# A hybrid encoder trunk on one core: GpSimd held back behind VectorE in the S5 prefix, and the mixer's head loop reordered

## The reference, cut to what matters

```python
proj = xn @ w_in                     # u (512), xm (512), v (512), o_pre (512)
y_a = s5_group(u, ...)               # 32 groups of 16 channels, 64 complex states each
q, k = per-head products of silu(conv4(xm)); v from proj; input and forget gates from q, k, v
h_t = mlstm_chunkwise(q, k, v, gates)         # 4 heads of 128
y_b = sigmoid(o_pre) * rmsnorm(h_t)
return concat(y_a, y_b) @ w_out
```

## Time and profile before

| | us |
|---|---|
| median of 3 runs (lowest, highest) | 1081.69 (1081.07, 1082.23) |
| the profiled execution's own time | 1083.43 |
| its span in the profile | 1081.6 |
| PE busy | 1068.1 |
| DVE, ACT, POOL busy | 639.7, 463.8, 188.1 |
| DMA, mean rate | 99 GB/s |

### The profile page before, as it was taken

One profiled execution on the slowest core, in us unless ns is written; L12 is line 12 of the kernel. 1 busy time (PEld: TensorE's weight loads), 2 busy tenths in 40 slices (PEclk: granted clock), 3 DMA queues, 4 the chain that ended last, 5 costly groups with the idle time before them and its releaser, 6 DMA issues.

```text
span 1081.6 us, 15533 instructions
## 1 busy us (share of the span) xinstructions
PE 1068.1 (99%) x5556; PEld 865.7 (80%) x5556; DVE 639.7 (59%) x874; ACT 463.8 (43%) x732; POOL 188.1 (17%) x243
## 2 busy tenths in 40 slices
PE   9999999999999999999999999999999999999997
PEld 7887578888888888888888777888888888888886
DVE  6799754566666666633334775656666666643332
ACT  6455565444434343422233565553444344422221
POOL 8999720400000000000000222310000000000000
PEclk9999999999999999999999999999999999999998
DMA  6551024232222222222324111223222222222322
GB/s 228 166 126 41 20 84 175 78 117 98 97 97 97 97 97 97 97 98 99 108 94 156 60 51 50 98 97 99 96 97 97 97 97 97 97 98 97 117 78 78
DMA packets 36459, 107.27 MB, mean 99 GB/s; under 512 B 7808, under 2 KB 10112, under 8 KB 36160
## 3 DMA queue, kind: packets, MB, share of 16 engines
q1 hardware_dynamic: 36416, 106.69, 29.7%
HBM read 102.09 MB, written 3.15 MB: 97 GB/s over the span
## 4 chain that ended last, share of the span: by engine, by line
PE 88%; DVE 2%; issue 1%; POOL 0%; ACT 0%; DVEq 0%
PE bank L1569 28%; PE bank L1570 27%; PE bank L1571 27%; PE bank L1593 1%; PE bank L1957 1%; PE bank L1934 1%; PE bank L1779 1%; PE bank L1714 1%; DVE wlo L1037 1%; PE bank L1707 0%; PE bank L1742 0%; PE bank L1736 0%; POOL pbuf L670 0%; DVE outb L1540 0%; DVE wbuf L1226 0%
## 5 line engine op out<-in xcount | busy, mean ns | idle before, releaser
L1569 PE MATMUL bank<-xhi,whi 128*128 128x512 f32 x960 | 376.5, 392 | 0.1
L1570 PE MATMUL bank<-xlo,whi 128*128 128x512 f32 x960 | 373.8, 389 | 0.0
L1571 PE MATMUL bank<-xhi,wlo 128*128 128x512 f32 x960 | 373.7, 389 | 0.0
L1037 DVE TENSOR_TENSOR wlo<-raw,whi 128x1024 fp32r<-128x1024 f32 x177 | 233.4, 1320 | 209.2 <-ACT whi L687 208.7
L687 ACT ACTIVATE whi<-raw 128x1024 fp32r<-128x1024 f32 x177 | 187.0, 1057 | 327.2 <-PE bank L1571 304.8
L1569 PEld LDWEIGHTS bank<-xhi,whi 128*128 128x128 f32 x960 | 180.3, 188 | 39.4 <-issue 0.8
L1571 PEld LDWEIGHTS bank<-xhi,wlo 128*128 128x128 f32 x960 | 180.3, 188 | 37.9
L1570 PEld LDWEIGHTS bank<-xlo,whi 128*128 128x128 f32 x960 | 180.4, 188 | 37.2 <-issue 0.3
L1569 PE MATMUL bank<-ahi,whi 128*128 128x512 f32 (+1 forms) x374 | 142.4, 381 | 0.0
L1570 PE MATMUL bank<-alo,whi 128*128 128x512 f32 (+1 forms) x374 | 142.2, 380 | 0.0
L1571 PE MATMUL bank<-ahi,wlo 128*128 128x512 f32 (+1 forms) x374 | 142.2, 380 | 0.0
(11 more groups left out here) (258 smaller groups left out, 1057.4 us busy)
## 6 DMA issues: line engine op xcount, KB each, us to landing
raw<-wstream SPq DMA_DIRECT2D x177, 512.0 KB, 3.2
xin<-xT SPq DMA_DIRECT2D x8, 256.0 KB, 5.4
raw<-wstream SPq DMA_DIRECT2D x8, 256.0 KB, 5.0
h<-xT SPq DMA_DIRECT2D x1, 2048.0 KB, 8.5
u_scratch<-uperm SPq DMA_DIRECT2D x1, 1024.0 KB, 5.5
uc<-u_scratch SPq DMA_DIRECT2D x8, 128.0 KB, 4.9
bandsb<-band SPq DMA_DIRECT2D x1, 1024.0 KB, 4.8
outT<-outb SPq DMA_DIRECT2D x2, 512.0 KB, 2.9
```

The costliest lines, as they stand in the source:

```text
L1037: V.tensor_tensor(wlo[:, t % RING, :], raw[:, t % RAWS, :], whi[:, t % RING, :].bitcast(f32), ALU.subtract).then_inc(lo_done, 1)
L1569: MM(dst, wh, rhi, start=start, stop=False)
L1570: MM(dst, wh, rlo, start=False, stop=False)
L1571: return MM(dst, wl, rhi, start=False, stop=stop)
```

## The change

- POOL waits for `lo_done` 17 (tiles 15 and 16 split) before it starts turning; and, in the forward turn of half 1, between `tprod` and `uprod`, for `hms_added` 1 (`head_sum(0)`).
- `toep` is cleared in three parts: blocks 4, 5 by ACT after head 1's decays (`toep_mid`), blocks 6, 7 and then 0 to 3 by POOL. SP issues the Toeplitz DMAs in the order 5, 4, 7, 6, 3, 2, 1, 0, each group behind its part.
- DVE adds the skip diagonal right after the copy of `ksb`, reading the bank; `peak` moves to bank 6 and the transposed `acol` to bank 5.
- `out_gate(1)` moves up between the forget scan and its use; `turned_half(0)`, `(1)` move up ahead of the `acol` copy, `turned_half(3)` behind `turned_half(2)`, `out_gate(3)` ahead of `weights(1)`.
- In the head loop `head_sum` follows `head_floor` and comes ahead of `weights`, and `mask_decay` comes behind `weights`; `split_lo` of tile 18 moves from the pass of head 1 to the pass of head 2, behind `weights` of the next head.
- PE projects tile 16 between `head_scores(0)` and `head_scores(1)`.
- At the start DVE, not ACT, rounds the first half of tile 0.

```diff
@@ SP
-        sp.wait_ge(toep_clear, 1)
-        for t in range(CH):
-            sp.dma_start(toep[(CH - 1 - t) * GCH:P, t, :, :],
-                         ksb[0:(t + 1) * GCH, :, :]).then_inc(toep_built, 16)
+        for ts, free, need in (((5, 4), toep_mid, 1), ((7, 6), toep_clear, 1), ((3, 2, 1, 0), toep_clear, 2)):
+            sp.wait_ge(free, need)
+            for t in ts:
+                sp.dma_start(toep[(CH - 1 - t) * GCH:P, t, :, :],
+                             ksb[0:(t + 1) * GCH, :, :]).then_inc(toep_built, 16)
@@ POOL
-        def turned_by(dst, src, back):
+        def turned_by(dst, src, back, after_sum=0):
             tt(tprod[:, :, :, :], src, turn[:, 0:1, :, :].to_broadcast([P, 2, PAIRS, HALF_CH]), ALU.mult)
+            if after_sum:
+                pool.wait_ge(hms_added, after_sum)
...
         pool.wait_ge(s5in_copied, 2)
+        pool.wait_ge(lo_done, T_QK + RING + 1)
...
-            turned_by(part[b], xr[:, b], False).then_inc(scan_done, 1)
+            turned_by(part[b], xr[:, b], False, after_sum=b).then_inc(scan_done, 1)
...
-        G.memset(toep[:, :, :, :], 0.0).then_inc(toep_clear, 1)
+        G.memset(toep[:, 6:8, :, :], 0.0).then_inc(toep_clear, 1)
+        G.memset(toep[:, 0:4, :, :], 0.0).then_inc(toep_clear, 1)
@@ ACT
-            A(whi[:, t, part], raw[:, t % RAWS, part], ACT.Copy).then_inc(hi_done if k % 2 else half_hi, 1)
+            if k:
+                A(whi[:, t, part], raw[:, t % RAWS, part], ACT.Copy).then_inc(hi_done if k % 2 else half_hi, 1)
...
+            if hd == 0:
+                act.wait_ge(scan_done, 1)
+                A(toep[:, 4:6, :, :], ones[:, 0:GCH].unsqueeze(1).unsqueeze(1).to_broadcast([P, 2, GROUPS, GCH]), ACT.Copy,
+                  scale=0.0).then_inc(toep_mid, 1)
@@ DVE
+        dve.wait_ge(half_in[0], 16)
+        V.tensor_copy(whi[:, 0, 0:512], raw[:, 0, 0:512]).then_inc(first_hi, 1)
...
-        V.tensor_copy(ksb[:, :, :], bank[6][:, :].rearrange("p (g i) -> p g i", i=GCH)).then_inc(k_copied, 1)
+        k_rows = bank[6][:, :].rearrange("p (g i) -> p g i", i=GCH)
+        V.tensor_copy(ksb[:, :, :], k_rows).then_inc(k_copied, 1)
+        dve.wait_ge(k_copied, 1)
+        dve.wait_ge(skip_set, 1)
+        V.tensor_tensor(ksb[0:GCH, :, :], k_rows[0:GCH], skipb[:, :].rearrange("p (g i) -> p g i", i=GCH),
+                        ALU.add).then_inc(k_final, 1)
...
                                       ALU.mult, ALU.add))
+        out_gate(1)
         settle()
...
-        out_gate(1)
+        turned_half(0)
+        turned_half(1)
         dve.wait_ge(acol_ready, 1)
...
         mask_decay(0)
-        turned_half(0)
-        turned_half(1)
-        dve.wait_ge(k_copied, 1)
-        dve.wait_ge(skip_set, 1)
-        V.tensor_tensor(ksb[0:GCH, :, :], ksb[0:GCH, :, :], skipb[:, :].rearrange("p (g i) -> p g i", i=GCH),
-                        ALU.add).then_inc(k_final, 1)
         out_gate(2)
         weights(0)
         turned_half(2)
+        turned_half(3)
+        out_gate(3)
         weights(1)
-        out_gate(3)
         weights(2)
-        turned_half(3)
         mask_decay(1)
...
             weights(SB * hd + 1)
             head_floor(hd - 1)
+            head_sum(hd - 1)
+            weights(SB * hd + 2)
             if hd + 1 < HEADS:
                 mask_decay(hd + 1)
-            head_sum(hd - 1)
-            weights(SB * hd + 2)
             head_scale(hd - 1)
             weights(SB * hd + 3)
-            if hd == 1:
-                split_lo(T_O + hd + RING)
             if hd + 1 < HEADS:
                 weights(SB * (hd + 1))
+            if hd == 2:
+                split_lo(T_O + 1 + RING)
             head_gate(hd - 1)
@@ PE
         broadcast_max(0)
+        head_scores(0)
+        project(T_O + 3, O_O + 3)
         pe.wait_ge(acol_copied, 1)
-        head_scores(0)
         head_scores(1)
-        project(T_O + 3, O_O + 3)
```

More of the change, by code:

```diff
@@ L262, in build @@
     half_in = [sem(f"half_in{t}") for t in range(RING)]
-    gain_in, half_hi, half_lo = sem("gain_in"), sem("half_hi"), sem("half_lo")
+    gain_in, first_hi, half_hi, half_lo = sem("gain_in"), sem("first_hi"), sem("half_hi"), sem("half_lo")
     hi_done, lo_done = sem("hi_done"), sem("lo_done")
@@ L310, in build @@
     radius_done, radius_set, min_done = sem("radius_done"), sem("radius_set"), sem("min_done")
-    arow_done = sem("arow_done")
+    arow_done, toep_mid = sem("arow_done"), sem("toep_mid")
     turned, turned_scan, carry_done, skip_set = (sem(n) for n in (
@@ L1059, in _ @@
             t, part = k // 2, slice(512 * (k % 2), 512 * (k % 2) + 512)
-            dve.wait_ge(hi_done if k % 2 else half_hi, t + 1)
+            dve.wait_ge(*((hi_done, t + 1) if k % 2 else (half_hi, t) if k else (first_hi, 1)))
             V.tensor_tensor(wlo[:, t, part], raw[:, t % RAWS, part], whi[:, t, part].bitcast(f32),
@@ L1194, in _ @@
         dve.wait_ge(kt_ready, 1)
-        V.tensor_copy(ksb[:, :, :], bank[6][:, :].rearrange("p (g i) -> p g i", i=GCH)).then_inc(k_copied, 1)
+        k_rows = bank[6][:, :].rearrange("p (g i) -> p g i", i=GCH)
[4 more added lines that the diff above has]
+                        ALU.add).then_inc(k_final, 1)
         dve.wait_ge(lnf_done, 1)
         dve.wait_ge(vtok_copied, HEADS)
-        lf_p, a_p, peak = bank[7][f_rows, :], bank[7][0:HEADS, :], bank[5][0:HEADS, :]
+        lf_p, a_p, peak = bank[7][f_rows, :], bank[7][0:HEADS, :], bank[6][0:HEADS, :]
         V.scalar_tensor_tensor(out=lf_p, in0=bank[0][f_rows, :], scalar=0.0, in1=lf,
@@ L1213, in _ @@
         V.tensor_tensor(fcum[:, :], peak, fcum[:, :], ALU.add).then_inc(sum_rows, 1)
-        out_gate(1)
+        turned_half(0)
+        turned_half(1)
         dve.wait_ge(acol_ready, 1)
-        V.tensor_copy(acol[:, :, :], bank[4][:, 0:SB * HEADS].rearrange("p (s h) -> p s h", h=HEADS)
+        V.tensor_copy(acol[:, :, :], bank[5][:, 0:SB * HEADS].rearrange("p (s h) -> p s h", h=HEADS)
                       ).then_inc(acol_copied, 1)
@@ L1604, in _ @@
                 pe.wait_ge(xhi_done, b + 1)
-                pe.wait_ge(hi_done if b % 2 else half_hi, t + 1)
+                pe.wait_ge(*((hi_done, t + 1) if b % 2 else (half_hi, t) if b else (first_hi, 1)))
                 for m in range(4):
@@ L1700, in _ @@
         for s in range(SB):
-            ins = transpose(bank[4][:, s * HEADS:(s + 1) * HEADS], arow[:, s * P:(s + 1) * P], HEADS)
+            ins = transpose(bank[5][:, s * HEADS:(s + 1) * HEADS], arow[:, s * P:(s + 1) * P], HEADS)
         ins.then_inc(acol_ready, 1)
```

## The result

| | before | after |
|---|---|---|
| median, us | 1081.69 | 1086.48 (1085.89 to 1087.73, 5 runs) |
| ratio, 95% interval | 1 | 1.0047 (1.0036 to 1.0059) |
| profiled execution: own time, span | 1083.43, 1081.6 | 1087.73, 1086.0 |

The change makes the kernel 4.8 us slower by the medians (3.9 to 6.4 by the interval). The forecast was 1081.4, its range ended at 1083.3. The traced execution of the changed kernel is the slowest of its five, 1.25 us over their median.

The account below looks back on a forecast made before the run. PE bounds the kernel, busy 1068.1 of 1081.6 us. Toeplitz start -1.95 plus clock +1.7 gives -0.25: profiled 1083.43 becomes 1083.2, and with the median 1.74 lower, 1081.4 us; range 1079.0 to 1083.3.

Parts of the forecast that it names:

- no wait at `broadcast_max`: Mixer prefix: PE's wait of 1.42 us goes whole, and with it the slow stretch that lost 1.7 us.
- the clock falling there: At the Toeplitz products: PE's stand of 2.9 us brings a 3.5 us stretch at half clock, 1.7 us lost.
- nothing for the first weights: Kernel start: DVE's copy makes PE's first matmul about 0.5 us earlier, lost again in the wait at 28.5; 0 taken.
- the last begins 4.45 later and, being the smallest now, lands in 2.0: Toeplitz DMAs: first issued at 139.5, last begins 4.45 us later and takes 2.0 us, landing at 145.9.
- The rule on ring order: Toeplitz DMAs: tile 20's 512 KB would delay blocks behind it; products start at most at 146.2, gain falls to 1.5 us.
- my own 145.7: Forecast start of the Toeplitz products, 1.95 us earlier than the 147.66 of the profiled execution.
- (a): Rival: PE's stand at the Toeplitz products costs no clock; 1079.7 us, chance 0.17.
- (b): Rival: the Toeplitz blocks are not late, so PE's whole 4.9 us gain passes on; 1076.8 us, chance 0.13.
- the 142.8 of my working: End of the head loop: PE ready for `s5_output(0)` at 142.8 where it was at 147.66, 4.9 us gained.
- (c): Rival: slower, the clock falls twice or for twice as long at the Toeplitz products, 3.4 us lost; 1083.2 us, chance 0.10.
- (d): Rival: POOL's remainder of head 0 comes ahead of tile 18's split, all lands 1.3 us later; 1082.7 us, chance 0.05.
- (e): Rival: POOL's wait is passed before DVE comes to its splits; ruled out beforehand, no time or chance given.

Follow-up runs that it names:

- g1: The kernel before, run again unchanged for a second trace: 1081.1 us, ratio 0.9998.
- e1: The changed kernel with the split of tile 18 back in the pass of head 1: 1078.42 us, ratio 0.9975.
- f4: The changed kernel, with SP waiting until all eight Toeplitz blocks have landed before it loads tile 21: 1086.39 us, ratio 1.0046.
- e2: The changed kernel, with the load of tile 20 behind the eight Toeplitz DMAs in SP's list, split still late: 1078.5 us, ratio 0.9975.
- e3: The changed kernel, with SP waiting until tile 20 has landed before it issues the first Toeplitz DMA: 1088.06 us, ratio 1.0068.
- e4: The changed kernel, with the Toeplitz blocks issued in the order 0 to 7, all behind the last clear: 1087.02 us, ratio 1.0048.
- f2: The kernel before, with only the split of tile 18 moved to the pass of head 2: 1088.71 us, ratio 1.0064.
- g2: The changed kernel, with SP waiting for tile 20 before the first Toeplitz block and for all blocks before loading tile 21: 1087.87 us, ratio 1.006.
- h1: The kernel before, with only the floor and sum of each finished head moved ahead of the next mask: 1080.87 us, ratio 0.9998.

## Why the prediction was wrong

**Right, by the trace (1.14 us taken off).** The forget sums start at 103.23 - 1.14 = 102.1, as said; the two splits take 2.36 together; no wait at `broadcast_max`, full clock behind it; head 1 at 125.5 (said 125.3), and later heads within 0.5 us of the working; the split of tile 18 done at 138.5 (said 139.1), the load of tile 20 ahead of the blocks, PE's longest wait moved to the Toeplitz products, the clock falling there, nothing for the first weights. The mechanism and its place were right. That the clock cost 1.5 to 1.7, with 1.7 said, is luck: the low clock lasted 6.8 us, not 3.5, and half of it fell into a wait of 6.9, not 2.9.

**The step that failed** is "the last begins 4.45 later and, being the smallest now, lands in 2.0". It began where I had it (145.05 - 1.14 = 143.9, said 143.95, with one issue of 1.00 us in place of 0.6 making up for an earlier start) and landed in 5.30: 3.3 us too few. I priced the blocks from the earlier trace rows, where tile 20 had landed before they were written, and stated that difference. I then took the 2.0 anyway, since tile 20 "should land at 142.5, earlier than the last block". That compared one arrival with another; the landings of the seven blocks before it (4.1 to 4.8 us) show that all of them were held up, the last one included. The rule on ring order, which I had priced at 0.5 us, pointed the right way, at a sixth of the size. Both ends of an unseen price should have gone into the range: one tile's 3.3 us on top of its end is 1086.6.

**The second error is the base.** I worked from one profiled execution and took its 1.74 us over the median for a constant. It was the slow stretch and the wait before it (g1's span is 2.3 us shorter). Against the median the changed kernel had no wait and no slow stretch to remove: the products stood at 145.26, so my own 145.7 was already 0.4 later, not 1.95 earlier. With that, the same working gives 1081.1 + 0.4 + 1.7 = 1083.2, and with the landing of 5.3 for 2.0 and 0.2 from my rounding down, 1086.7. Measured: 1086.48. So close a match is in part luck, since the 5.3 is from an execution of 1087.73, 1.25 us over the median; its late start (29.68 at tile 4, where the traces of e1 and f4 have 28.77 and 29.27) may be 0.4 to 0.9 of that. As spans it closes to 0.1: 1079.3 (g1) to 1086.0 is 6.7; the products' start moved by 5.1 us (0.7 of which was there at tile 4 already, 28.97 to 29.68), and the clock costs 1.5.

**The rivals.** (a) fell: the clock did fall. (b) held in the kernels that free the blocks (e1, e2), where I had 1076.8 and the runs show 1078.4; the difference is again the base (145.26 to the 142.8 of my working is 2.5 us, and 2.7 were measured). (c), slower, came out in sign and in the clock: it was low for twice as long as in the earlier trace rows, from 147 to 153.8. But half of that lay inside the wait, so it cost 1.5 and not 3.4, and most of the loss is the wait of 6.9, which (c) does not have. (d) did not occur: the split came ahead of POOL's remainder. (e) did not occur: POOL stood 3.28 us for the split.

**Open.** In all six traces in which PE stands at the Toeplitz products (after, e3, e4, f2, f4, g2) one of the eight issues on SP takes 0.70 to 2.23 us in place of 0.6, and in the other eight traces none does. What makes it is not shown. A candidate is the packet of 16 KB that the profile lists as "q8 instruction": in e3, e4, f2 and g2 one was under way during the slow issue (143.75 to 145.50 in e4), in after and f4 it came behind the slow issue, while blocks were still landing (146.22 and 144.77), and in the other eight traces all blocks had landed before it. It may also have held up the last block after the change. Nor is it shown how much of the 5.30 belongs to the one traced execution.

## What to carry to other kernels

Moving work that frees a buffer moves the load behind it, and everything that stands behind that load in the issuing engine's list; here one split of 1.2 us, moved by one pass, decided between -0.25% and +0.5%. When a transfer is to start beside another that the trace has only shown by itself, price it with the whole of the other's time as the upper end. And before counting a wait or a slow stretch as a saving, ask whether it is in the median: where the profiled execution is over it by about the size of that very stretch, it may not be. Last, an edit that brings PE back to work a little earlier gains less than it seems while the clock is low: f4 and e4 started the products 2.2 and 1.5 us earlier and took the same time.

## What the runs showed of the hardware

- The same two DVE splits took 2.36 us with POOL held back, 4.53 (g1) or 8.68 (before) beside POOL's two-input operations; a 128 x 4 sum took 0.16 or 2.27. The Trainium skill (SBUF — State Buffer, "SBUF: two separate sides") has the port pair of the two engines as a lock held for a whole instruction. The 6.45 of the first split is longer than any one POOL operation there (2.35 and 2.4): by that rule it stood through more than one, and the traces agree, as it started during `skipb` and ended 1.1 us behind `uprod`.
- PE at rest since about 143.5 had its clock fall near 147 (after). The length of a stand alone does not say whether the clock falls: one of 1.42 us had a slow stretch of 3.5 us behind it, one of 0.80 us too (h1), and others of 0.80 and 1.13 us had none (g1).
- With PE at rest for 5.0 to 7.6 us the low clock lasted 6.8 us in six traces of six, and did not end sooner where work came back sooner.
- An SP issue took 0.6 us in most cases, up to 2.2 us in single ones (e4).
